# Expert loop and routing of a two-layer backbone: row stores moved to GpSimd without padding rows, indices signalled apart, one load and the totals moved

## What is computed

```python
lg = h @ moe_w_group + moe_b_group              # 4 groups
gi = argmax(lg); gw = max(softmax(lg))
le = (h @ moe_w_expert + moe_b_expert) of group gi   # 4 experts in the group
tv, ti = top_k(le, 2); tw = softmax(tv) * gw
x += gate2 * sum over the two experts e:  tw_e * (silu(h @ w1g_e) * (h @ w1u_e)) @ w2_e
```

## Time and profile before

| | us |
|---|---|
| median of 3 runs (1900.81 to 1906.64) | 1901.49 |
| the profiled execution | 1910.62 |
| its span | 1908.8 |
| PE busy | 1657.5 (87%) |
| VectorE busy | 1198.3 (63%) |
| ScalarE busy | 893.7 (47%) |
| GpSimd busy | 425.7 (22%) |

### The profile page before, as it was taken

The page is one execution under the profiler, slowest core; times in us unless marked ns, Lnnn a source line. Parts: engine busy times, 40 slices in busy tenths (PEclk is TensorE's granted clock), DMA queues, the critical chain, the costliest instruction groups (busy, mean ns, idle before and its releaser), DMA issues.

```text
span 1908.8 us, 34493 instructions
## 1 busy us (share of the span) xinstructions
PE 1657.5 (87%) x13277; PEld 1112.8 (58%) x13277; DVE 1198.3 (63%) x1900; ACT 893.7 (47%) x1468; POOL 425.7 (22%) x418
## 2 busy tenths in 40 slices
PE   6799889999989974888778998899999999388776
PEld 4478766777665542434455886677776556244336
DVE  4595455777537546877665925477773584787754
ACT  3322455666541123777533226466664211377653
POOL 0033243222241201212102324322222221111102
PEclk7899999999999986999859999999999999699995
DMA  8555235532327465999624732222223553399954
GB/s 296 181 197 171 68 132 182 183 104 73 115 104 255 157 253 190 350 380 365 241 112 144 246 125 87 77 98 73 73 73 127 197 195 120 126 362 371 373 210 166
DMA packets 191106, 350.71 MB, mean 184 GB/s; under 512 B 15477, under 2 KB 98934, under 8 KB 190710
## 3 DMA queue, kind: packets, MB, share of 16 engines
q1 hardware_dynamic: 181647, 319.58, 47.8%
q0 software_dynamic: 7776, 28.32, 4.0%
q10 hardware_dynamic: 1543, 0.88, 0.2%
HBM read 287.72 MB, written 61.01 MB: 183 GB/s over the span
## 4 chain that ended last, share of the span: by engine, by line
PE 65%; DVE 12%; DMA 9%; ACT 5%; issue 5%; DVEq 2%; SPq 1%; another core or an unknown queue 1%; ACTq 0%; POOL 0%; POOLq 0%
PE PS L431 38%; PE PS L438 10%; DMA wf<-in_moe_w 5%; PE PS L1055 3%; PE PS L1039 3%; DMA arena<-in_moe_w 3%; PE PS L857 2%; PE PS L813 1%; DVE arena L2363 1%; PE PS L839 1%; PE PS L823 1%; ACT arena L1439 1%; DVE hpart L1862 1%; DVE scratch L1853 1%; DMA wf<-in_w_out 1%
## 5 line engine op out<-in xcount | busy, mean ns | idle before, releaser
L1722 POOL TENSOR_TENSOR wlo<-wf,whi 128x256 f16<-128x256 f32 (+1 forms) x268 | 278.1, 1071 | 911.4 <-ACT whi L1366 911.4
L431 PE MATMUL PS<-hpart,whi 128*128 128x320 f16 x2048 | 426.5, 301 | 15.5 <-ACT arena L1439 14.5
L431 PE MATMUL PS<-hpart,wlo 128*128 128x320 f16 x1024 | 308.0, 301 | 0.0
L431 PE MATMUL PS<-whi,hpart 128*128 128x256 f16 (+2 forms) x1568 | 298.4, 291 | 5.9 <-DVE scratch L1983 3.6
L431 PEld LDWEIGHTS PS<-hpart,whi 128*128 128x128 f16 x2048 | 191.5, 98 | 104.4 <-issue 34.9
L431 PE MATMUL PS<-wlo,hpart 128*128 128x256 f16 (+2 forms) x784 | 225.7, 290 | 0.0
L431 PEld LDWEIGHTS PS<-whi,hpart 128*128 128x128 f16 x1568 | 151.9, 98 | 65.2 <-issue 24.1
L2363 DVE TENSOR_TENSOR arena<-arena 128x2048 f16<-128x2048 f32 x66 | 149.5, 2288 | 36.0 <-ACT arena L1617 35.8
L2159 DVE TENSOR_REDUCE stat<-PS 128x1 f32<-128x640 f32 (+1 forms) x160 | 110.7, 713 | 80.3 <-PE PS L1039 77.6
L1439 ACT ACTIVATE arena<-PS,pcol 128x320 f32<-128x320 f32 x128 | 67.4, 527 | 173.3 <-PE PS L431 167.9
L1617 ACT CAST arena<-arena 128x2048 f16<-128x2048 f32 x66 | 123.4, 1897 | 41.2 <-DMA arena<-in_moe_w 28.1
(11 more groups left out here) (348 smaller groups left out, 2809.6 us busy)
## 6 DMA issues: line engine op xcount, KB each, us to landing
arena<-in_moe_w SPq DMA_DIRECT2D x66, 1024.0 KB, 9.9
arena<-in_w_ada SPq DMA_DIRECT2D x40, 1024.0 KB, 7.4
wf<-in_moe_w SPq DMA_DIRECT2D x36, 1024.0 KB, 9.8
wf<-in_w_gate SPq DMA_DIRECT2D x32, 1024.0 KB, 5.5
g_rows<-arena SPq DMA_DIRECT2D x128, 160.0 KB, 1.8
wf<-in_w_in SPq DMA_DIRECT2D x18, 1024.0 KB, 7.7
y_rows<-scratch SPq DMA_DIRECT2D x34, 512.0 KB, 8.8
arena<-g_rows SPq DMA_DIRECT2D x24, 640.0 KB, 5.1
```

The lines of the kernel that those rows point to most:

```text
L431: ins = pe.matmul(out, st, mv, start=first and n == 0, stop=last and n == 2)
L1722: ins = pool.tensor_tensor(lo[:, a:b], wf[j][:, a:b], hi[:, a:b], ALU.subtract)
```

## The change

1. **Stores by POOL, padding left out.** SP's `store` is gone. POOL's new `rows_to` waits for `my_ready`, adds the row numbers of the chunk into a register column and issues an indirect store to `y_rows`. Padding rows get a number beyond the table's end, and the bounds check leaves them out. Gathers from chunk 3 on leave padding out the same way (`idxall`); the first three use `idx3`, which stays in bounds, so that both buffers hold finite numbers. On partition 0 padding stays in bounds in both. Two tiny gathers at the program's start (`spared`) replace a preset of the stores' semaphores by VectorE.
2. **Indices signalled apart.** The list holds token - 1024 instead of the token, so that 0 means padding. `idx_ready` is signalled with `idx3` and `idxall`; PE's loop start and POOL's first gathers wait for it. `slots_ready` follows with the store's row numbers, and `route_ready`, now only the number of turns and `cexp`, last. PE, ACT and DVE read the number of turns just before their loops, behind the first chunks' work; DVE's router weights (`rcol`) go there too. `ran_before` on PE goes ahead of the rank matmuls, on DVE ahead of the output projection's residuals.
3. **Totals on PE.** Five more accumulating matmuls of a tile's `cum` by ones add the earlier tiles' totals to the ranks; the column block behind the tiles holds the totals. VectorE's five steps and its add go. All five `row_tile` stand ahead of the wait for them.
4. **`ada_load(l + 1, 7)`** is issued ahead of the row stores.

The diff, cut to its core:

```diff
@@ SP
                 sp.wait_ge(*xraw_ready(l, KC))
                 load(slice(1, 2), 1, 2)
+                if ahead:
+                    ada_load(l + 1, 7)
                 for tile in range(TILES):
                     sp.wait_ge(*rows_whole(l, tile + 1))
                     sp.dma_start(t["h2_rows"][P * tile:P * tile + P, :], htok[:, tile, :]).then_inc(rows_out.sem, 16)
                 if ahead:
-                    ada_load(l + 1, 7)
                     params_load(sp, l + 1)
...
-                def store(c, j, row):
-                    sp.wait_ge(my_ready.sem, past + (c + 2))
-                    sp.dma_start(t["y_rows"][ds(row, P), :] if not isinstance(row, int) else t["y_rows"][row:row + P, :],
-                                 ybuf[j]).then_inc(y_out[j].sem, 16)
@@ PE
-                pe.matmul(bank(4)[:, 128:208], before, cum.rearrange("p t e -> p (t e)"), start=True, stop=True)
-                pe.matmul(bank(4)[:, 256:336], ones[:, :], cum.rearrange("p t e -> p (t e)"), start=True, stop=True
-                          ).then_inc(cnt_done.sem, 1)
+                pe.matmul(bank(4)[:, 128:224], before, cumz, start=True, stop=False)
+                for tile in range(TILES):
+                    n = TILES - tile
+                    ins = pe.matmul(bank(4)[:, 144 + 16 * tile:224].rearrange("p (r e) -> p r e", r=n), ones[:, :],
+                                    cum[:, tile, :].rearrange("p (o e) -> p o e", o=1).to_broadcast([P, n, EXPERTS]),
+                                    start=False, stop=tile == TILES - 1)
+                ins.then_inc(cnt_done.sem, 1)
@@ POOL
                     pool.indirect_dma_start(out=dst, out_offset=None, in_=t["h2_rows"],
-                                            in_offset=bass.IndirectOffsetOnAxis(ap=index, axis=0)).then_inc(done.sem, 16)
+                                            in_offset=bass.IndirectOffsetOnAxis(ap=index, axis=0),
+                                            bounds_check=TOK - 1, oob_is_err=False).then_inc(done.sem, 16)
+                def rows_to(c, j):
+                    pool.wait_ge(my_ready.sem, past + (c + 2))
+                    pool.tensor_tensor(rowi[:, j:j + 1], slotrow[:, ds(c, 1)], zero1[:, :], ALU.add)
+                    pool.drain()
+                    pool.indirect_dma_start(out=t["y_rows"],
+                                            out_offset=bass.IndirectOffsetOnAxis(ap=rowi[:, j:j + 1], axis=0),
+                                            in_=ybuf[j], in_offset=None,
+                                            bounds_check=CHUNKS * P - 1, oob_is_err=False).then_inc(y_out[j].sem, 16)
...
+                rows_next(3, 1)
+                rows_next(4, 0)
+                rows_to(0, 0)
+                with pool.Fori(1, p + 1) as i:
                     for n in range(2):
-                        pool.wait_ge(ht_done.sem, past + (i * 2 + (2 + n)))
-                        pool.tensor_tensor(idxi[:, 1 - n:2 - n], idxall[:, ds(i * 2 + (3 + n), 1)], zero1[:, :], ALU.add)
-                        pool.drain()
-                        rows_from(xg[1 - n], idxi[:, 1 - n:2 - n], xg_in[1 - n])
+                        rows_next(i * 2 + (3 + n), 1 - n)
+                        rows_to(i * 2 + (n - 1), 1 - n)
+                for c in range(1, 5):
+                    rows_to(p * 2 + c, c % 2)
@@ DVE
-                for tile in range(3):
+                for tile in range(TILES):
                     row_tile(tile)
                 dve.wait_ge(*cnt_done(l, 1))
...
-                for tile in range(TILES):
-                    dve.tensor_tensor(acc[:, tile + 1, :], acc[:, tile, :], bank(4)[:, 256 + 16 * tile:272 + 16 * tile],
-                                      ALU.add)
-                    dve.drain()
-                dve.tensor_tensor(cum, bank(4)[:, 128:208].rearrange("p (t e) -> p t e", t=TILES), acc[:, 0:5, :], ALU.add)
...
-                for tile in range(3, TILES):
-                    row_tile(tile)
...
+                dve.wait_ge(*list_done(l, 1))
+                found = bank(5, CHUNKS + 2)
+                dve.tensor_scalar(idx3, found[:, 0:3], 1024.0, float(TOK - 1), ALU.add, ALU.min)
+                dve.tensor_scalar(idxall, found, limit, 1024.0, ALU.min, ALU.add).then_inc(idx_ready.sem, 1)
+                dve.scalar_tensor_tensor(out=padslot, in0=found, scalar=0.0, in1=bc(padding, [P, CHUNKS + 2]),
+                                         op0=ALU.is_equal, op1=ALU.mult)
+                dve.drain()
+                dve.tensor_tensor(slotrow, padslot, ownslot, ALU.add).then_inc(slots_ready.sem, 1)
...
-                dve.tensor_scalar(loopi[:, 1:2], loopf[:, 1:2], -2.0, None, ALU.add)
-                dve.wait_ge(*list_done(l, 1))
-                dve.tensor_copy(idxall, bank(5, CHUNKS + 2)).then_inc(route_ready.sem, 1)
+                dve.tensor_scalar(loopi[:, 1:2], loopf[:, 1:2], -2.0, None, ALU.add).then_inc(route_ready.sem, 1)
```

More of the change, by code:

```diff
@@ L281, in build @@
         cexp = smalli[:, 12:12 + CHUNKS + 1]
+        idx3, slotrow = smalli[:, 38:41], smalli[:, 41:41 + CHUNKS + 2]
+        spare = small[:, 276 + CHUNKS + 2:448]
+        tokneg, padding, limit = spare[:, 68:73], spare[:, 73:74], spare[:, 74:75]
+        ownslot, padslot = spare[:, 75:75 + CHUNKS + 2], spare[:, 102:102 + CHUNKS + 2]
+        rowi = smalli[:, 129:131]
         loopf = sb("loopf", [P, 3])
@@ L1713, in _ @@
         def _(pool):
+            pool.wait_ge(*set_ready(0, 5))
+            for j in range(2):
+                pool.indirect_dma_start(out=spared[:, 4 * j:4 * j + 4], out_offset=None, in_=t["k_tie"],
+                                        in_offset=bass.IndirectOffsetOnAxis(ap=zero1[:, :], axis=0)).then_inc(y_out[j].sem, 16)
             for l in range(LAYERS):
@@ L1815, in _ @@
                 dve.nop().then_inc(s.sem, 1)
-            for s in y_out:
-                dve.nop().then_inc(s.sem, 16)
             dve.nop().then_inc(comb_ready.sem, TILES)
@@ L2389, in first_max @@
                     dve.drain()
+                dve.memset(cumz[:, 16 * TILES:], 0.0)
+                dve.wait_ge(*route_in(l, 16))
+                dve.tensor_scalar(tokneg, tokid, -1024.0, None, ALU.add)
+                dve.tensor_scalar(padding, tokid[:, 0:1], 1.0, 4096.0, ALU.min, ALU.mult)
+                dve.tensor_scalar(ownslot, iota[:, 0:CHUNKS + 2], float(P), None, ALU.mult)
+                dve.drain()
+                dve.tensor_scalar(limit, padding, float(TOK - 1 - 1024), None, ALU.add)
+                dve.tensor_scalar(ownslot, ownslot, tokid[:, 0:1], None, ALU.add)
                 lg = route[:, :, 0:4]
@@ L2411, in _ @@
                 dve.tensor_tensor(cum, ohm[:, 0:5, :], ohm[:, 5:10, :], ALU.add).then_inc(hot_ready.sem, 1)
-                for tile in range(3):
+                for cs in csum:
+                    dve.memset(cs[:, 0:8], 0.0)
+                for tile in range(TILES):
                     row_tile(tile)
@@ L2437, in count @@
                     dve.drain()
-                count(nch, acc[:, 5, :], steps[:, 1:5], ALU.is_gt, EXPERTS, 4)
+                count(nch, totals, steps[:, 1:5], ALU.is_gt, EXPERTS, 4)
                 dve.tensor_copy(csum[0][:, 8:24], nch)
@@ L2543, in _ @@
                 part_low(0, 0, 6)
+                dve.wait_ge(*rexp_ready(l, 1))
+                dve.tensor_reduce(rcol[:, 3, :], ex5[:, :, 0:4], AX_X, ALU.add)
+                dve.tensor_scalar(rcol[:, 4, :], ex5[:, :, 4], 1.0, None, ALU.add)
+                dve.drain()
+                dve.tensor_tensor(rcol[:, 5, :], rcol[:, 3, :], rcol[:, 4, :], ALU.mult)
+                dve.drain()
+                dve.reciprocal(rcol[:, 3, :], rcol[:, 5, :])
+                dve.drain()
+                dve.tensor_tensor(rcol[:, 4, :], rcol[:, 3, :], ex5[:, :, 4], ALU.mult)
+                dve.drain()
+                for n in (3, 4):
+                    dve.tensor_scalar(rcol[:, n + 2, :], rcol[:, n, :], 1.0 / A_SCALE, None, ALU.mult)
+                dve.wait_ge(started.sem, 1)
+                dve.wait_ge(*route_ready(l, 1))
+                p = pairs_now(dve)
                 with dve.Fori(0, p + 1) as i:
```

80 lines of the change are left out of this document (35 added, 45 removed).

## The result

The changed kernel takes **1981.43 us** (median of four, 1974.87 to 1983.46) against 1901.29 us for the kernel before beside it: a ratio of 1.0409, 95% interval 1.0378 to 1.0439. It is 80 us slower where 38 us faster was forecast, and 98 us above the top of the range. Its profiled execution took 1981.27 us, with a span of 1979.4 us.

What follows compares the result with a forecast made beforehand. The prediction took DMA bytes to bound the expert loops. Layer 0: 15 - 2 + 14 - 2 = 25 us; layer 1: 3.5 - 2 + 14 - 2 = 13.5; 1901.5 - 38.5 = 1863 us, range 1852 to 1883.

Steps and rivals of the forecast that it cites:

- so POOL keeps up: Expert loop: gather and store, some 3.3 us each, make 6.6 us of a 10.1 us period; moving stores costs nothing.
- A late gather has two periods in hand: Expert loop: a gather issued late behind its wait still has two chunk periods before it is needed; no cost.
- So the loop is bound by bytes: Expert loop: DMA engines full at share 1.00, so leaving out padding rows gains 14 us a layer.
- rival 1's second form: Expert loops: PE, VectorE and ScalarE bind at once; loops give 0 to 7 us each, 1877 to 1891; rival 1 17%.
- Start of layer 0, 15 us: Before layer 0's loop: earlier adaLN load and indices at 725 start first transposes 14 to 16 us earlier, 15 taken.
- Layer 1, 3.5 us: Before layer 1's loop: indices ready near 1654.8 start PE's filler earlier; 3.5 us gained, 0 if the gather takes 8.
- What comes back, 2 us a layer: After the first chunks' work: router weights' last operations and register loads now cost 2 us a layer (0 to 3).
- Store at the loop's end, 2 us lost a layer: End of each expert loop: POOL's last store lies on the path; 2 us lost a layer (0.7 to 2.4).
- The slower one (3): Expert loop: POOL becomes the bound if a store keeps it over 7.9 us; at 9.5 us, time 1935; 8%.
- Rival 4: Expert loops: stored row costs twice a gathered one, or loads gain too; 20 us a loop, time 1851; 7%.
- rival 2: Expert loops: POOL's added issues and adds hold up VectorE, half the loops' gain goes; sum 24, time 1877; 10%.

Runs made afterwards that it cites:

- experiment 5: Changed kernel with POOL's two loop drains replaced by its own semaphore and the gather waiting for chunk c - 2's transposes: 1880.54 us, again 1880.06 us.
- experiments 6: Changed kernel, drains kept, with only the gather's wait set back to the transposes of chunk c - 2: 1962.42 us.
- experiment 1: Changed kernel with POOL's two loop drains replaced by a semaphore of its own, the gather's wait left at chunk c - 1: 1888.50 us.
- experiment 10: Changed kernel with stores back on SP, all rows moved, the gather's wait at chunk c - 2 and its drain kept: 1878.92 us.
- experiment 3: Kernel before with one POOL drain added behind each pair of the ten gathers that follow the loop: 1929.28 us.
- experiment 2: Changed kernel, drains kept, with the padding offset set to 0 so that all rows are moved: 1994.18 us.
- experiment 7: The kernel of experiment 5 with the padding offset set to 0 so that all rows are moved: 1885.41 us.

## Why the prediction was wrong, step by step

- **"A gather costs POOL 1.80 us of issue, 0.68 us for the index add ahead of it and 0.83 us between them"; "Two of them make 6.6 us of a period of 10.1, so POOL keeps up."** This is the step that failed. The 0.83 us between them is what a drain takes when nothing of POOL's is in flight. When something is, it takes until that has landed. The kernel before has one gather a chunk, which lands in 7 to 9.4 us of a period of 11.2. So its drain waits too, ahead of 5 of the 11 issues from 785 to 900, but never for more than 2 us beyond the 0.8. The changed kernel has two DMAs a chunk, and the sum that counts is 5.3 + 8.2 us of landing and twice 0.85, not 6.6 us of POOL's work: 15.2 us, against a period of 11.2 before. Without the drain (experiment 5) the same two DMAs a chunk go out within a period of 10.7.
- The trace of before already had it, in the timeline of POOL:
```profile
835.85 0.95 POOL L1769 DMA_INDIRECT hpart<-h_rows,wulo  x1 [0.82 <-issue]
842.21 1.05 POOL L1787 TENSOR_TENSOR wulo<-wulo,zero 128x1 int32<-128x1 int32 x1 [5.41 <-PE PS L1185]
846.05 0.95 POOL L1769 DMA_INDIRECT hpart<-h_rows,wulo  x1 [2.80 <-issue]
852.19 0.19 POOL L1787 TENSOR_TENSOR wulo<-wulo,zero 128x1 int32<-128x1 int32 x1 [5.18 <-PE PS L1185]
854.64 2.49 POOL L1769 DMA_INDIRECT hpart<-h_rows,wulo  x1 [2.26 <-issue]
```
  The gap before an issue is 0.82, 2.80, 2.26 us. The gather of 835.85 landed 9.4 us on, at 845.25, and the next went out at 846.05; that one landed 7.8 us on, at 853.85, and the next went out at 854.64. I took a group's mean issue and its least gap for a price; the earlier trace rows has the idle time, 16.1 us over 12 gathers or 1.34 us each, which is already more than the 0.83 I used, and the difference was a wait.
- **"A late gather has two periods in hand."** It has one: the changed wait is for the transposes of chunk c - 1, not c - 2. With the drain this costs 19 us, without it 8 (experiments 6 and 5 against the changed kernel and 1), each with some us of noise.
- **"So the loop is bound by bytes", 14 us a layer.** It fell. Bytes and DMA time went as worked out (31.7 us by the forecast's 9.8 ns a row, 31 found), but the share of 1.00 was no ceiling. This step failed too: repaired as in experiment 5, the kernel gains 1.4% over the one before, and experiment 10 gains as much with all rows moved. What held it is close to rival 1's second form, PE, VectorE and ScalarE; the chain in experiment 5 shows a ring of weight load, split and buffer, and PE works 105.7 of 120 us, 9.5 of a period of 10.8. Which of them ends last is argued from these rows and not shown; a load that lands sooner, or a third weight buffer, was not tried.
- **Start of layer 0, 15 us.** Held: 14.5 us, in part by luck. The load is issued at 704.60, near the 702 forecast, and no longer makes PE wait, as the timeline shows beside the 17.92 us in the earlier trace rows:
```profile
704.60 0.47 SPq L547 DMA_DIRECT2D hpart<-in_w_ada  x1
...
716.25 3.64 PE L854 MATMUL PS<-hpart,bias 128*32 128x512 f32 x16
...
727.69 0.24 DVE L2525 TENSOR_SCALAR wulo<-PS,wulo 128x27 int32<-128x27 f32 x1
...
729.13 1.04 POOL L1774 DMA_INDIRECT hpart<-h_rows,wulo  x1 [0.86 <-issue]
...
733.53 1.09 PE L1183 MATMUL PS<-ident,hpart 128*128 128x128 f32 x8 [0.40 <-DMA hpart<-h_rows,wulo]
```
  The indices came at 727.9 and not at 725. The router's last count in layer 0 came 2.0 us later than before (711.60 for 709.57); the load is now in flight beside it, but whether it is the cause was not tried. The gather made up for part: 4.4 us, the short end of the range for it.
- **Layer 1, 3.5 us.** Held: 2.9. **What comes back, 2 us a layer**: from the first transposes to the third, where it would show, +0.4 and +2.5 us. **Store at the loop's end, 2 us lost a layer**: in layer 0 POOL's next work starts 4.3 us after the last copy's end (974.10 to 978.43) where it was 3.0, so 1.3 us are the store's; the stretch lost 3.1, with POOL's last drains in it. In layer 1 the stretch from the last transposes to the end is 1.5 us shorter, so no loss is seen.
- **The rivals.** The slower one (3) had the right engine, side and condition, a store that keeps POOL for more than 7.9 us, but the wrong cause: not the software's work on 128 rows but the wait for both landings. At a period of 15.2 a store keeps it for 15.2 - 3.3 = 11.9 us; its price by its own formula, 14 x 4 x 2 = 112 us less 10.5, is 101 us where 80 were lost. It got 8%, and was priced at 9.5 us, since I looked for a slow issue and not for a wait. **Rival 4** gave a stored row up to twice a gathered one's cost: both kinds together took 9.6 ns a row, so no.
- **VectorE and POOL, rival 2.** The Trainium skill (SBUF — State Buffer, section "SBUF: two separate sides") has VectorE and POOL hold each other up. Here the changed kernel's POOL adds took 0.20 us each in layer 0's loop (770 to 890) and its issues 1.0 to 3.0, against waits of 4 to 7 us for landings, so this was not what decided. In experiment 5, with both DMAs on POOL and VectorE busy, adds take up to 1.5 us on the mean: POOL is held up. VectorE is not seen to be: its commonest operation in the loop, the low part of a weight piece, takes 2.29 us on the mean in the kernel before, in the changed one and in experiment 5.

## What to carry to other kernels

Ask of every drain or other full stop on an engine that also issues DMAs what is in flight when it is reached: its price is the landing of the slowest of these, it is small only while each DMA has landed by then, and in this loop a second DMA on the same engine turned it into the period. Where only one result has to be visible, let that instruction raise a semaphore and wait for it. And a DMA busy share of 1.00 does not say that bytes bind: taking bytes away and seeing the period stay is what says that they don't.

## What the runs showed of the hardware

- A drain on POOL ends 0.8 to 0.9 us after the last of POOL's own earlier DMAs has landed (experiment 3: 0.30 us between two gathers without it, 4.9 to 5.6 with it). With an own semaphore and a tiny add in its place 0.8 us pass from the index add's end (785.39) to the issue (786.20) in the rows of experiment 1, with a gather 2 us old in flight; a drain with nothing to wait for takes 0.83. In experiment 5 the tiny add ahead of a gather is itself held up, 1.4 us on the mean.
- Indirect DMAs of 128 rows of 4 KB, beside weight loads: in the changed kernel's loop (DMA share 0.76) gathers land in 5.1 to 5.9 us and stores in 7.5 to 9.7, and with no row left out (experiment 2, share 0.79) the medians are the same within 0.2 us. In the loop of the kernel before (share 1.00) gathers take 6.9 to 9.4 us.
- Rows left out by the bounds check keep their packets and free their bytes: 13.24 MB less took 31 us less of all 16 engines. For 3235 rows of 4 KB that is 9.6 ns a row, as the 9.8 worked out before.
- The DMA share can read 1.00 at 366 GB/s in one kernel and 1.03 at 391 to 399 GB/s in another that moves the same rows and weights (experiment 7, 770 to 890 and 1660 to 1780).
- While PE waited for late gathers its granted clock averaged 0.87 and 0.86 over the loops, against 0.95 and 0.96 before and 0.97 in experiment 5.
